# Gate and up blocks of four SwiGLU FFNs: two blocks one after the other, or chunk by chunk together

## The chip, the cores and the metric

The kernel runs on one NeuronCore of one Trainium2 chip. The metric is the device time of one launch in microseconds (us), as the median of the runs shown. The profile is of one execution.

## The reference

The computation is two layers over a state of 512 tokens (256 latent, 256 context) by 1024, in fp32. Each layer is a half-step SwiGLU FFN, a mixer of attention, gated convolution and pooling, and another half-step FFN. In the last FFN only the 256 latent tokens are left. What the change touches is the first product of each FFN:

```python
D_MODEL = 1024; SEQ = 256; CTX_LEN = 256; DEPTH = 2; D_FF = 2816

def _swiglu(x, w_gu, w_down):
    g, u = jnp.split(x @ w_gu, 2, axis=-1)
    return (jax.nn.silu(g) * u) @ w_down

for l in range(DEPTH):
    mod = (silu_c @ w_mod[l] + b_mod[l]).reshape(B, N_MOD, D_MODEL)   # shifts, scales and gates
    ...
    h = h + 0.5 * m[2][:, None] * _swiglu(_modulate(_rms(h, norm_w[l, 0]), m[0], m[1]),
                                          ffn1_w_gu[l], ffn1_w_down[l])
    ...                                                               # mixer, then the second FFN
```

The product `silu_c @ w_mod[l]`, the modulation, is also computed inside the kernel, in the shadow of the FFNs.

## The kernel before, in words

**Data.** The state is held transposed, 1024 features as 8 chunks of 128 partitions, tokens along the free axis (`w` = 512, or 256 in the last FFN). All products are fp32 made of three reduced-precision ones: a weight block and the activations are each split into a high part and the rest (`whi`, `wlo`, `xh`, `xl`), and the helper `three` (lines 1159 to 1163) issues high × high, high × low, low × high into one PSUM bank. A matmul has one 128 × 128 weight tile and up to 512 moving columns.

**Weights.** They come as a stream of 320 blocks of 512 KB, in the order in which they are used. SP loads block n into `raw` (line 332) once block n − 5 is finished (`block_done`, ring of 5). `raw` and `wlo` are the same memory. ACT copies it to `whi` (line 396), which waits for block n − 4 to be finished, since `whi` has 4 slots. DVE then subtracts, giving `wlo` (line 683). PE waits for that with `lo_done`.

**An FFN.** Its first stage, gate/up, has 44 blocks: gate block 2j and up block 2j+1 are pair j (j from 0 to 21). `column_block` (line 1165) multiplies one block: 8 chunks of three matmuls, 24 in a row into one bank, and signals `block_done` with the last. Blocks 0 to 2 go through `first_blocks` as the normalised activations arrive, the other 41 through `column_block`, in banks 0, 1, 2, 3 in turn. Before the first block of a pair PE waits with `mul_done` until the pair two before has been read out of its two banks. When both blocks of pair j are finished, ACT applies SiLU to the gate bank (line 409) and DVE multiplies with the up bank (`hidden`, line 731). ACT makes the high part of the product `ah` (line 414) and DVE the low part `al` (`hidden_low`, line 738). The second stage, down, has 22 blocks (`down`, line 1260): each goes through four banks, three matmuls in a bank and then the next, with the same moving columns. The third bank of its first block waits for `hidden` of the last pair (line 1267).

**The modulation.** 36 units of half a modulation vector. A unit's weights come in four loads of 512 KB on POOL's queue (line 354), two in flight. DVE multiplies and accumulates them for both condition vectors in four parts (`mod_pair`, lines 704 and 708, four instructions of 512 columns each), then 8 small matmuls of PE sum over the partitions (`mod_sums`, line 1222, waiting for `mod_acc`), which are recorded as 16. In the first three FFNs (f = 0, 1, 2) the gate/up stage carries 11, 11 and 9 units: unit i − 1 of the stage is summed inside block 4i + 1, before its third chunk.

**The order around it** is written out by hand for each engine. Within one pair j it is:

```python
# ACT: split_next(2j), hidden_high(j-1), split_next(2j+1), silu(j)
# DVE: split_next(2j), hidden_low(j-1), mod_pair(unit, e), split_next(2j+1), hidden(j), mod_pair(unit, e+1)
```

`split_next(n)` splits block n + 4. A unit takes two such iterations of DVE (its parts e = 0, 1 and then 2, 3), so its last part stands behind `hidden` of pair 2i − 1. Engines follow this order whatever is ready.

Of the kernel before, what the change touches and what calls it, by code (L numbers as in the profile page):

```python
# [28 lines left out]
DC = D // P  # L29
# [16 lines left out]
RING = 5  # L46
SPL = 4
GU = 2 * FC
# [27 lines left out]
FIRST = 3  # L76
# [21 lines left out]
def program(nc, wstream, wmod, cols, x_t, out):  # L98
    with ExitStack() as ctx:
        def sb(name, shape, dt=F32):  # L100
            return ctx.enter_context(nc.sbuf_tensor(name, shape, dt))

        def sem(name):
            return ctx.enter_context(nc.semaphore(name))
# [5 lines left out]
        wlo = sb("wlo", [P, RING, TILES, P], F32R)  # L110
        whi = sb("whi", [P, SPL, TILES, P], F32R)
        h = sb("h", [P, DC, T])
        xh = sb("xh", [P, DC, T], F32R)
        xl = sb("xl", [P, DC, T], F32R)
# [52 lines left out]
        ps = ctx.enter_context(nc.psum_tensor("ps", [P, 8, T], F32))  # L167

        def col(name, i=0, n=1):
            a = COLS[name][0] + i  # L170
            assert i + n <= COLS[name][1]
            return K[:, a:a + n]
# [6 lines left out]
        lo_done = sem("lo_done")  # L179
        block_done = sem("block_done")  # L180
# [24 lines left out]
        mul_done = sem("mul_done")  # L205
# [38 lines left out]
        def width(m):  # L244
            return T if m < 5 else S

        def streams(m):
            return width(m) // S
# [4 lines left out]
        def staggered(m):  # L253
            return 0 < m < 5
# [23 lines left out]
        def xstep(m, d, s):  # L278
            return XT[m] + DC * s + d + 1
# [28 lines left out]
        def unit_steps(u):  # L308
            return 2 * DC * (u - START_UNITS)
# [848 lines left out]
        def _(pe):  # L1158
            def three(out_ap, hi_w, lo_w, hi_x, lo_x, start, stop):

                pe.matmul(out_ap, hi_w, hi_x, start=start, stop=False)  # L1161
                pe.matmul(out_ap, hi_w, lo_x, start=False, stop=False)  # L1162
                return pe.matmul(out_ap, lo_w, hi_x, start=False, stop=stop)  # L1163

            def column_block(n, bank, a, b, last=True, between=None):


                pe.wait_ge(lo_done, n + 1)
                for c in range(DC):
                    if c == 2 and between:  # L1170
                        between()
                    ins = three(ps[:, bank, a:b], whi[:, n % SPL, c, :], wlo[:, n % RING, c, :],
                                xh[:, c, a:b], xl[:, c, a:b], c == 0, c == DC - 1)
                if last:
                    ins.then_inc(block_done, 1)
                return ins

            def first_blocks(m, n):


                for s in range(streams(m)):
                    a, b = s * S, (s + 1) * S
                    last = s == streams(m) - 1
                    for c in range(DC):
                        pe.wait_ge(xl_done, xstep(m, c, s))
                        for q in range(2):
                            if c == 0:
                                pe.wait_ge(lo_done, n + q + 1)
                            ins = three(ps[:, FIRST_BANKS[m][q], a:b], whi[:, (n + q) % SPL, c, :],
                                        wlo[:, (n + q) % RING, c, :], xh[:, c, a:b], xl[:, c, a:b],  # L1190
                                        c == 0, c == DC - 1)
                            if last and c == DC - 1:
                                ins.then_inc(block_done, 1)
                    if staggered(m) and s == 0:
                        norm_stat(m, 1)
                    column_block(n + 2, FIRST_BANKS[m][2], a, b, last)
# [19 lines left out]
            def mod_sums(f, u):  # L1216

                pe.wait_ge(mod_acc, unit_steps(u + 1))
                for v in range(2):
                    r = 2 * (u - UNIT_AT[f][0]) + v  # L1220
                    for j in range(HN // P):
                        ins = pe.matmul(ps[32 * j:32 * j + 32, ROWS_BANK, 0:P], col("pick", 31 - r, 32),  # L1222
                                        macc[:, v, j * P:(j + 1) * P], start=r == 0,
                                        stop=u + 1 == SET_ENDS[f] and v == 1)
                ins.then_inc(mod_sum, 1)

            def mod_turn(f):

                pe.wait_ge(mod_rows, f + 1)
                pe.transpose(ps[:, TURN_BANK, 0:P], mrows[:, :], col("ident", 0, P)).then_inc(mod_turned, 1)  # L1230
# [11 lines left out]
            def ffn(l, st):  # L1242
                f = 2 * l + (st == 2)
                m = 3 * l + st
                n0 = PER_LAYER * l + (0 if st == 0 else FFN + MIX)
                w = width(m)
                u0, nu = UNIT_AT.get(f, (0, 0))
                F0 = FC * f

                first_blocks(m, n0)  # L1250
                for i in range(GU // 4):
                    for e in range(FIRST if i == 0 else 0, 4):
                        if e % 2 == 0 and i:

                            pe.wait_ge(mul_done, F0 + 2 * i + e // 2 - 1)
                        sums = e == 1 and 1 <= i <= nu
                        column_block(n0 + 4 * i + e, e, 0, w,
                                     between=(lambda u=u0 + i - 1: mod_sums(f, u)) if sums else None)

                def down(hf, b, order, banks, a=0, z=w, first=0, final=HALF - 1, parts=0):  # L1260

                    n = n0 + GU + HALF * hf + b
                    pe.wait_ge(lo_done, n + 1)
                    for r, d in order:
                        if hf == 0 and b == 0 and r == 0:

                            pe.wait_ge(mul_done, F0 + FC - (d < 2))
                        src = (2 * b + r) * T
                        ins = three(ps[:, banks[d], a:z], whi[:, n % SPL, 4 * r + d, :],
                                    wlo[:, n % RING, 4 * r + d, :], ah[:, src + a:src + z], al[:, src + a:src + z],  # L1270
                                    b == first and r == 0, b == final and r == 1)
                        if r == 1 and d < parts:
                            ins.then_inc(part_done, 1)
                    return ins

                by_row = [(r, d) for r in range(2) for d in range(4)]
                by_bank = [(r, d) for d in range(4) for r in range(2)]
                pairs = [(r, d) for g in range(2) for r in range(2) for d in (2 * g, 2 * g + 1)]
                for b in range(HALF):

                    pe.wait_ge(al_done, F0 + 2 * b + 2)
                    down(0, b, pairs if b == 0 else by_row, DN_BANKS[0]).then_inc(block_done, 1)
                    if nu == GU // 4 and b == 1:
                        mod_sums(f, u0 + nu - 1)
                    if f == 0 and b == 6:
                        mod_sums(f, LATE_UNIT)
                    if nu and b == 8:
                        mod_turn(f)
                if nu:

                    pe.wait_ge(mod_col, SET_ENDS[f])
                    pe.wait_ge(mod_rows, f + 1)
                if not staggered(m + 1):
                    for b in range(HALF - 1):
                        down(1, b, by_row, DN_BANKS[1]).then_inc(block_done, 1)
                    down(1, HALF - 1, by_bank, DN_BANKS[1], parts=3).then_inc(block_done, 1)
                    return
                main = HALF - TAIL
                for b in range(main):
                    down(1, b, by_row, DN_BANKS[1], final=main - 1).then_inc(block_done, 1)  # L1300

                pe.wait_ge(h_done, H0[m] + JOINT)
                for b in range(main, HALF - 1):
                    down(1, b, by_row, DN_BANKS[0], 0, S, first=main)
                down(1, HALF - 1, by_bank, DN_BANKS[0], 0, S, first=main, parts=4)

                pe.wait_ge(h_done, H0[m] + 2 * JOINT)
                for b in range(main, HALF - 1):
                    down(1, b, by_row, DN_BANKS[1], S, T, first=main).then_inc(block_done, 1)
                    if b == main:  # L1310
                        norm_stat(m + 1, 0)
                down(1, HALF - 1, by_bank, DN_BANKS[1], S, T, first=main, parts=3).then_inc(block_done, 1)
# [291 lines left out]
```

## Time and profile before

| | |
|---|---|
| time, median of 3 runs | 1734.02 us (1733.18 to 1736.59) |
| span of the profiled execution, first to last instruction | 1731.9 us |
| PE matmuls | busy 1670.1 us (96%), 9475 instructions |
| VectorE (DVE) | busy 1085.4 us (63%) |
| ScalarE (ACT) | busy 610.1 us (35%) |
| DMA | 249.42 MB, mean 144 GB/s |
| granted clock of TensorE | 0.988 of full speed |

The times of the runs do not say which of them was profiled; its span lies 2.1 us under their median. PE is TensorE, its weight loads are recorded apart (PEld) and overlap the matmuls. Matmuls overlap each other, so the distance between their starts is what one costs, not its duration. In the rows, L12 is line 12 of the kernel, and "[idle before <-releaser]" is how long the engine had nothing to do before the row and what ended that.

### The profile page before, as it was taken

The numbers are of one execution on the slowest core, as the hardware profiler recorded it, in microseconds if no ns is written. First come the engines' busy times: TensorE is split into PE (matmuls) and PEld (weight loads), VectorE is DVE, ScalarE is ACT, GpSimd is POOL, SyncE is SP. The second block draws the span as 40 slices with busy tenths as digits, with TensorE's granted clock in tenths as the row PEclk, the third lists the DMA queues.
The fourth block names the chain that finished last, engine by engine and source line by source line (L and its number), as shares of the span: only waits on it lengthen the run. The fifth ranks groups of instructions, "written<-read, shape, count | busy, mean of one in ns | idle before, by whom it ended". The sixth has DMA issues, their size and how long they took to land.

```text
span 1731.9 us, 23714 instructions
## 1 busy us (share of the span) xinstructions
PE 1670.1 (96%) x9475; PEld 1416.9 (82%) x9475; DVE 1085.4 (63%) x1652; ACT 610.1 (35%) x917; POOL 84.9 (5%) x150
## 2 busy tenths in 40 slices
PE   3999999999999999999999999999999999979999
PEld 1888887889877897888888887888888987979999
DVE  2877777435668577787753387777423477755544
ACT  3422222123545452222222152222222365544432
POOL 0000000000000100000000000000000000000000
PEclk9999999999999999999999999999999999989999
DMA  9355555432221225565543245555323332335554
GB/s 362 123 182 189 183 187 188 154 96 86 89 71 49 86 98 169 184 195 184 182 157 98 74 142 171 186 193 179 105 96 97 97 99 80 131 119 183 183 168 149
DMA packets 69881, 249.42 MB, mean 144 GB/s; under 512 B 7440, under 2 KB 8464, under 8 KB 69776
## 3 DMA queue, kind: packets, MB, share of 16 engines
q1 hardware_dynamic: 51344, 180.83, 31.8%
q0 software_dynamic: 18432, 67.12, 11.8%
q8 instruction: 75, 1.23, 0.3%
q14 instruction: 30, 0.25, 0.0%
HBM read 246.87 MB, written 1.05 MB: 143 GB/s over the span
## 4 chain that ended last, share of the span: by engine, by line
PE 90%; DVE 4%; DMA 2%; issue 2%; ACT 1%; SPq 1%; POOLq 0%; POOL 0%; DVEq 0%; ACTq 0%
PE ps L1161 29%; PE ps L1162 28%; PE ps L1163 28%; DMA raw<-wstream 2%; DVE shared_a L708 1%; PE ps L1222 1%; PE ps L1364 1%; ACT whi L396 1%; PE ps L1396 1%; PE ps L1324 1%; DVE wlo L683 1%; SPq L326 1%; PE ps L1378 0%; SPq L322 0%; DVE nmax L1006 0%
## 5 line engine op out<-in xcount | busy, mean ns | idle before, releaser
L683 DVE TENSOR_TENSOR wlo<-raw,whi 128x1024 fp32r<-128x1024 f32 x320 | 393.7, 1230 | 576.0 <-ACT whi L396 574.4
L1161 PE MATMUL ps<-xh,whi 128*128 128x512 f32 (+1 forms) x1956 | 692.6, 354 | 8.6 <-DVE xl L793 5.1
L1162 PE MATMUL ps<-xl,whi 128*128 128x512 f32 (+1 forms) x1956 | 676.2, 346 | 0.0
L1163 PE MATMUL ps<-xh,wlo 128*128 128x512 f32 (+1 forms) x1956 | 675.6, 345 | 0.0
L396 ACT ACTIVATE whi<-raw 128x1024 fp32r<-128x1024 f32 x320 | 338.6, 1058 | 910.8 <-PE ps L1163 776.9
L1161 PEld LDWEIGHTS ps<-xh,whi 128*128 128x128 f32 x1956 | 373.7, 191 | 66.5 <-issue 12.8
L1162 PEld LDWEIGHTS ps<-xl,whi 128*128 128x128 f32 x1956 | 374.0, 191 | 46.2 <-issue 3.8
L1163 PEld LDWEIGHTS ps<-xh,wlo 128*128 128x128 f32 x1956 | 373.5, 191 | 45.1
L708 DVE SCALAR_TENSOR_TENSOR shared_a<-wm,cs,shared_a 128x512 f32<-128x512 f32 x448 | 307.6, 746 | 0.0
L1161 PE MATMUL ps<-ah,whi 128*128 128x512 f32 (+1 forms) x800 | 274.6, 343 | 3.7 <-DVE shared_b L731 3.7
L1162 PE MATMUL ps<-al,whi 128*128 128x512 f32 (+1 forms) x800 | 273.0, 341 | 0.0
L1163 PE MATMUL ps<-ah,wlo 128*128 128x512 f32 (+1 forms) x800 | 272.9, 341 | 0.0
L1161 PEld LDWEIGHTS ps<-ah,whi 128*128 128x128 f32 x800 | 152.4, 190 | 22.9 <-DVE shared_b L731 5.2
L1163 PEld LDWEIGHTS ps<-ah,wlo 128*128 128x128 f32 x800 | 152.4, 190 | 17.0
L1162 PEld LDWEIGHTS ps<-al,whi 128*128 128x128 f32 x800 | 152.5, 191 | 16.7
L354 POOL DMA_DIRECT2D wm<-wmod x126 | 66.8, 530 | 892.1 <-DVEq L711 884.5
L461 ACT ACTIVATE shared_a<-h 128x256 f32<-128x256 f32 (+1 forms) x64 | 31.6, 498 | 81.7 <-DVE h L750 73.4
L750 DVE SCALAR_TENSOR_TENSOR h<-ps,gcol,h 128x256 f32<-128x256 f32 x104 | 45.6, 477 | 20.8 <-PE ps L1163 20.7
L731 DVE TENSOR_TENSOR shared_b<-shared_b,ps 128x512 f32<-128x512 f32 (+1 forms) x88 | 54.1, 615 | 2.5 <-ACT shared_b L409 2.5
L738 DVE TENSOR_TENSOR al<-shared_b,ah 128x512 fp32r<-128x512 f32 (+1 forms) x88 | 54.4, 619 | 1.5 <-ACT ah L414 1.2
L477 ACT ACTIVATE xh<-shared_b,modc 128x256 fp32r<-128x256 f32 x88 | 42.2, 504 | 31.1 <-DVE shared_b L785 31.1
L414 ACT ACTIVATE ah<-shared_b 128x512 fp32r<-128x512 f32 (+1 forms) x88 | 49.5, 563 | 9.9 <-DVE shared_b L731 9.9
(106 smaller groups left out, 798.9 us busy)
## 6 DMA issues: line engine op xcount, KB each, us to landing
raw<-wstream SPq DMA_DIRECT2D x320, 512.0 KB, 3.5
wm<-wmod POOLq DMA_DIRECT2D x128, 512.0 KB, 4.7
wm<-wmod SPq DMA_DIRECT2D x3, 2048.0 KB, 20.5
h<-x_t SPq DMA_DIRECT2D x1, 2048.0 KB, 11.4
wm<-wmod SPq DMA_DIRECT2D x2, 1024.0 KB, 20.4
out_t<-h SPq DMA_DIRECT2D x8, 128.0 KB, 2.7
K<-cols SPq DMA_DIRECT2D x1, 939.0 KB, 13.8
K<-cols SPq DMA_DIRECT2D x1, 268.5 KB, 3.0
```

Of the source, the lines that this page charges most:

```text
L354: pool.dma_start(wm[:, c, :, :].rearrange("p a n -> p (a n)"), wmod[bass.ds(i * 2 + c, 1)].rearrange("a p n -> p (a n)"))\
L396: act.activation(whi[:, n % SPL, :, :].rearrange("p a b -> p (a b)"), raw[:, n % RING, :], ACT.Copy)\
L414: act.activation(ah[:, j * T:j * T + w], af[:, j % 2, 0:w], ACT.Copy).then_inc(ah_done, 1)
L477: act.activation(xh[:, d, s * S:(s + 1) * S], xt[:, (g - 1) % 4, :], ACT.Identity, bias=modc[:, N_MOD * l + 3 * st, d, s:s + 1]).then_inc( ...
L683: dve.tensor_tensor(wlo[:, n % RING, :, :].rearrange("p a b -> p (a b)"), raw[:, n % RING, :], whi[:, n % SPL, :, :].rearrange("p a b -> p ...
L708: ins = dve.scalar_tensor_tensor(acc, src, sc, acc, ALU.mult, ALU.add)
L731: dve.tensor_tensor(af[:, j % 2, 0:w], sil[:, j % 2, 0:w], ps[:, gu_bank(f, 2 * j + 1), 0:w], ALU.mult)\
L738: dve.tensor_tensor(al[:, dst], af[:, j % 2, 0:w], ah[:, dst].bitcast(F32), ALU.subtract)\
L750: ins = dve.scalar_tensor_tensor(h[:, d, v * S:(v + 1) * S], ps[:, bank, v * S:(v + 1) * S], gcol[:, m, d, v:v + 1], h[:, d, v * S:(v + 1) ...
L1161: pe.matmul(out_ap, hi_w, hi_x, start=start, stop=False)
L1162: pe.matmul(out_ap, hi_w, lo_x, start=False, stop=False)
L1163: return pe.matmul(out_ap, lo_w, hi_x, start=False, stop=stop)
```

## The change

In the gate/up stage, blocks 4 to 43 are no longer multiplied one after the other. The new function `column_pair` takes a gate block and its up block together. For each of the 8 chunks it goes through `xh` with `whi`, `xh` with `wlo`, `xl` with `whi`, and issues each for the gate block into bank `bank` and for the up block into bank `bank + 1`. Both blocks must be split before it starts (`lo_done` at n + 2). The last two matmuls of the pair signal `block_done`, one each. The sums of a modulation unit stand ahead of chunk 5 of the pair (30 of its 48 matmuls before them), where they stood ahead of the third chunk of its second block (24 + 6 before them). Block 3 stays a `column_block`, and the other engines' programs are as before.

```diff
+                def column_pair(n, bank, between=None):
+                    pe.wait_ge(lo_done, n + 2)
+                    for c in range(DC):
+                        if c == 5 and between:
+                            between()
+                        for x, lo in ((xh, False), (xh, True), (xl, False)):
+                            for q in range(2):
+                                wt = wlo[:, (n + q) % RING, c, :] if lo else whi[:, (n + q) % SPL, c, :]
+                                ins = pe.matmul(ps[:, bank + q, 0:w], wt, x[:, c, 0:w],
+                                                start=c == 0 and x is xh and not lo, stop=c == DC - 1 and x is xl)
+                                if c == DC - 1 and x is xl:
+                                    ins.then_inc(block_done, 1)
+
                 first_blocks(m, n0)
-                for i in range(GU // 4):
-                    for e in range(FIRST if i == 0 else 0, 4):
-                        if e % 2 == 0 and i:
-
-                            pe.wait_ge(mul_done, F0 + 2 * i + e // 2 - 1)
-                        sums = e == 1 and 1 <= i <= nu
-                        column_block(n0 + 4 * i + e, e, 0, w,
-                                     between=(lambda u=u0 + i - 1: mod_sums(f, u)) if sums else None)
+                column_block(n0 + FIRST, FIRST, 0, w)
+                for i in range(1, GU // 4):
+                    for e in (0, 2):
+
+                        pe.wait_ge(mul_done, F0 + 2 * i + e // 2 - 1)
+                        sums = e == 0 and i <= nu
+                        column_pair(n0 + 4 * i + e, e,
+                                    between=(lambda u=u0 + i - 1: mod_sums(f, u)) if sums else None)
```

## Rows read from the trace of the kernel before

**Rows 1.** The page, part 4: shares of the chain that ended last, by engine.

```profile
PE 90%; DVE 4%; DMA 2%; issue 2%; ACT 1%; SPq 1%; POOLq 0%; POOL 0%; DVEq 0%; ACTq 0%
```

**Rows 2.** Timeline of PE, a block with sums: start us, us, engine, line, operation, tiles, count.

```profile
168.96 0.39 PE L1161 MATMUL ps<-xh,whi 128*128 128x512 f32 x1
...
170.41 0.64 PE L1222 MATMUL ps<-shared_a,K 128*32 128x128 f32 x16
...
175.20 0.39 PE L1161 MATMUL ps<-xh,whi 128*128 128x512 f32 x1
```

**Rows 3.** Timeline of DVE, then ACT, beside the block of rows 2.

```profile
164.87 1.23 DVE L683 TENSOR_TENSOR wlo<-raw,whi 128x1024 fp32r<-128x1024 f32 x1 [0.96 <-ACT whi L396]
...
166.61 2.73 DVE L708 SCALAR_TENSOR_TENSOR shared_a<-wm,cs,shared_a 128x512 f32<-128x512 f32 x4
...
170.31 1.23 DVE L683 TENSOR_TENSOR wlo<-raw,whi 128x1024 fp32r<-128x1024 f32 x1 [0.97 <-ACT whi L396]
...
169.22 1.06 ACT L396 ACTIVATE whi<-raw 128x1024 fp32r<-128x1024 f32 x1 [3.89 <-PE ps L1163]
```

**Rows 4.** Timeline of DVE in the first FFN, while it works without a gap.

```profile
69.31 1.23 DVE L683 TENSOR_TENSOR wlo<-raw,whi 128x1024 fp32r<-128x1024 f32 x1
...
71.05 2.73 DVE L708 SCALAR_TENSOR_TENSOR shared_a<-wm,cs,shared_a 128x512 f32<-128x512 f32 x4
...
73.93 1.23 DVE L683 TENSOR_TENSOR wlo<-raw,whi 128x1024 fp32r<-128x1024 f32 x1
...
75.08 0.68 DVE L731 TENSOR_TENSOR shared_b<-shared_b,ps 128x512 f32<-128x512 f32 x1
...
75.67 2.73 DVE L708 SCALAR_TENSOR_TENSOR shared_a<-wm,cs,shared_a 128x512 f32<-128x512 f32 x4
```

**Rows 5.** Timeline of PE: first sums of three FFNs, and the block after each.

```profile
78.46 1.08 PE L1222 MATMUL ps<-shared_a,K 128*32 128x128 f32 x16 [4.15 <-DVE shared_a L708]
...
84.84 0.39 PE L1161 MATMUL ps<-xh,whi 128*128 128x512 f32 x1
...
660.22 1.08 PE L1222 MATMUL ps<-shared_a,K 128*32 128x128 f32 x16 [3.79 <-DVE shared_a L708]
...
667.47 0.39 PE L1161 MATMUL ps<-xh,whi 128*128 128x512 f32 x1
...
1039.87 0.64 PE L1222 MATMUL ps<-shared_a,K 128*32 128x128 f32 x16 [3.77 <-DVE shared_a L708]
...
1046.25 0.39 PE L1161 MATMUL ps<-xh,whi 128*128 128x512 f32 x1
```

**Rows 6.** Windows: column blocks, down blocks, narrow FFN. Stretch, length, busy (xcount), PEclk, DMA share, GB/s.

```profile
1237.00:1257.00 20.00, 20.00 (x90) 16.57 (x89) 6.98 (x8) 6.25 (x8) 0.00 (x0) 1.00 0.33 103
314.00:338.00 24.00, 24.00 (x108) 19.87 (x107) 14.10 (x18) 4.24 (x4) 2.12 (x4) 1.00 0.52 176
1610.00:1650.00 40.00, 40.00 (x336) 40.00 (x335) 21.42 (x28) 18.87 (x28) 0.00 (x0) 1.00 0.56 183
```

**Rows 7.** The chain in order of time, last block of the narrow gate/up stage.

```profile
1658.94 3.94 DMA raw<-wstream
```

**Rows 8.** DMA issues from 90 to 290: count, KB each, median us to landing.

```profile
raw<-wstream SPq DMA_DIRECT2D x36, 512.0 KB, 3.5
wm<-wmod POOLq DMA_DIRECT2D x36, 512.0 KB, 4.8
```

**Rows 9.** Windows behind the pauses that end at 660.22 and 1665.60.

```profile
662.00:664.00 2.00, 2.00 (x7) 1.54 (x6) 2.00 (x5) 0.00 (x0) 0.00 (x0) 0.50 0.83 254
...
1666.00:1668.00 2.00, 2.00 (x11) 2.00 (x11) 0.43 (x1) 0.00 (x0) 0.00 (x0) 0.50 0.00 0
```

**Rows 10.** Timeline of PE: the matmuls that end other pauses.

```profile
302.25 0.50 PE L1161 MATMUL ps<-ah,whi 128*128 128x512 f32 x1 [0.35 <-DVE shared_b L731]
...
1546.34 0.38 PE L1161 MATMUL ps<-xh,whi 128*128 128x256 f32 x1 [0.95 <-DVE shared_b L731]
...
1665.60 0.51 PE L1161 MATMUL ps<-ah,whi 128*128 128x256 f32 x1 [2.37 <-DVE shared_b L731]
```

## The prediction

> **What bounds the kernel now.** I read the chain that ended last first [rows 1]: 90% of it is TensorE (PE), and no other engine has more than 4%. So a matmul saved is time saved, and a pause of PE is time lost. Whether PE pauses depends on the engines that feed it, so next I read one steady period of the gate/up stage, where most of the changed code runs. The block that carries the modulation sums [rows 2]: its first matmul is at 168.96, the sums (L1222) come at 170.41, which is 1.45 after it, and the next block begins at 175.20, 4.79 after the sums. Beside it [rows 3], DVE's splits start at 164.87 and 170.31, 5.44 apart, as the blocks of PE end: 24 matmuls of 0.2267. The last four multiply-adds of the unit (L708, `mod_pair`) run from 166.61 for 2.73, to 169.34. The sums may start then, and PE reaches them at 170.41: a slack of 1.07 us. That number is what the change has to live with. Two delays for later: ACT starts its split 0.26 after the next block's first matmul (169.22 − 168.96), and DVE 1.09 after ACT (170.31 − 169.22).
>
> Three first units already show this wait failing. DVE when it works without a gap [rows 4]: from the split at 69.31 to the modulation pair at 71.05 it is 1.74, on to the next split 2.88, to `hidden` (L731) 1.15, to the second modulation pair 0.59, and that lasts 2.73, to 78.40. The sums come 0.06 later, at 78.46 [rows 5], and PE had been idle for 4.15.
>
> **The matmuls themselves.** The change issues the same 48 matmuls for a pair of blocks in another order, with a weight load each as before. Could the order make them cheaper? In the down stage, every third matmul already goes to another bank with the same moving columns as the one before it (`xh` or `ah` of L1163, then of L1161, with d changed). In the windows of rows 6 the column blocks start 90 matmuls in 20.00 us and the down blocks 108 in 24.00: 0.222 us each in both. So neither alternating banks nor sharing columns is worth anything that this trace can show, and I enter 0. The bounds: a gain down to pure streaming at the granted 2.4 GHz (512 columns, 0.2133; 256 columns, 0.1067) would be 0.0134 on 2,880 matmuls (120 blocks of 24 in the three wide FFNs) and 0.0123 on 960 (40.00/336 = 0.119 [rows 6] less 0.1067), so 38.6 + 11.8 = 50 us. For a loss I take the opposite of that as the end, 0.01 on each, 38 us; rows 6 lie at neither.
> The Trainium skill (TensorE: Matmul & The Clock Gate, "Back-to-back issue gap") gives N/2.4 + 2.5 ns, 216 ns at 512 columns and 109 at 256; this trace has 227 and 119. If the new order brought the kernel to the page's gap, an estimate from it is 2,880 × 11 ns + 960 × 10 ns = 41 us of gain; nothing in rows 6 points there, and the sum does without it.
>
> **When blocks are finished.** Before, gate block 2j of pair j ended 5.44 before up block 2j+1. Now both end together; the gate block's last matmul is the second to last of the pair. What waits for `block_done` of 2j is ACT's split of block 2j+4, DVE's split behind it, and SP's load of block 2j+5. All of them start nearly a block later, and everything behind them in DVE's fixed order moves as well: `hidden_low`, the first modulation pair, the second split, `hidden`, the second modulation pair. Let T be the first matmul after pair j. ACT starts the first split at T + 0.26 − 0.227 = T + 0.03, DVE at T + 1.12. By rows 4 the first modulation pair then starts at T + 2.86, the second split at 5.74, `hidden` at 6.89, the second modulation pair at 7.48, and it ends at 10.21. Before, only one split, `hidden` and the second pair lay behind T: T was 168.96 − 5.44 = 163.52 and the end 169.34, T + 5.82.
>
> Is anything else late? The load of 2j+5 is issued at T − 0.06 and takes 3.5 to 3.94 [rows 7, 8], so it is there by T + 3.9; ACT then lets DVE in at T + 5.0, before 5.74, hidden by 0.7. The next pair but one needs both its blocks split (5.74 + 1.23 = 6.97) and `hidden` of j (6.89 + 0.68 + 0.06 = 7.63) by T + 10.88: hidden with 3.2 to spare. If that cover goes, the narrow FFN shows the price (term 4). DVE's whole iteration (10.21) fits in the 10.88 of a pair too.
>
> **Term 1, the sums.** They now stand ahead of chunk 5 of pair 2i, 30 matmuls after T: T + 6.80, plus the 0.09 that rows 2 have at the same place (1.45 − 6 × 0.2267), T + 6.89, which is where they stood before (5.44 + 1.45). They need the modulation pair that ends at 10.21, so they start at T + 10.27: PE pauses 3.38. How often: units with sums in the loop are i = 1 to 10, 1 to 10 and 1 to 9, 29 in all; the first of each FFN waits already and does not change, since blocks 0 to 3 and their splits keep their times. 26 new pauses × 3.38 = 87.9 us.
>
> **Term 2, the clock.** After such pauses the granted clock is at 0.50, the 1.2 GHz level: so behind the one that ends at 660.22, and behind the one of the narrow FFN that ends at 1665.60 [rows 9, 10]. From the start of the sums to the next block normally takes 4.79. In rows 5 it takes 84.84 − 78.46 = 6.38, 667.47 − 660.22 = 7.25 and 1046.25 − 1039.87 = 6.38: dearer by 1.59, 2.46, 1.59, mean 1.88. Those pauses were about 4 us and mine is 3.4, but the one of 2.37 at 1665.60 dropped the clock too; behind the 0.95 of 1546.34 the blocks came at full rate. So each of my 26 is charged 1.88: 48.9 us. Bounds: 0 and 2.46 each (0 and 64).
>
> **Term 3, the end of each gate/up stage.** The third bank of the first down block waits for `hidden` of the last pair. Before, it started at 302.25 [rows 10] with 0.35 of idle time, counted from the modelled end of a matmul, 0.39 − 0.227 = 0.16 behind its turn; so 0.51 late, and the 12 matmuls ahead of it take 2.72: T + 3.23. Now it starts at T + 7.63: 4.40 more, and the pause of 4.9 costs the clock too: 6.3, in two FFNs. In the third, where the last pair has no modulation pair beside it, the load sets it: T + 3.9, DVE 1.11 later, `hidden` at 6.15 to 6.83, PE at 6.9: 3.7 + 1.9 = 5.6. In the narrow one the load is issued at T + 0.04 and takes 3.94 [rows 7]; DVE at 5.09, `hidden` at 6.24 and taken as 0.41 long (between half and all of the 0.68 of rows 4), PE at T + 6.71. Before, T was 1658.94 − 0.16 + 24 × 0.119 = 1661.64 and PE went on at 1665.60, T + 3.96: 2.7 more, its clock drop is there already. Sum 12.6 + 5.6 + 2.7 = 20.9 us.
>
> **Term 4, the narrow FFN.** A pair of 256 columns takes 48 × 0.119 = 5.71. Pair j+2 needs `hidden` of j (its bank's reader) at T + 6.71, and its turn comes at T + 5.71: 1.00 of pause. After it the next pair is in time, so the pause comes before every second pair, 9 times: 9.0 us, without a clock drop at that length [rows 10].
>
> **Sum.** 87.9 + 48.9 + 20.9 + 9.0 = 166.7 on a span of 1731.9: 1898.6. The median of the runs shown is 2.1 above this span, so 1901.
>
> **Rivals.** (a) The pauses come, but are too short for the clock: less 29 × 1.9 = 55 us, 1846. For it: 3.4 is shorter than the three of about 4. Against it: 2.4 was enough once. (b) The loads come in twos and hold each other up. The narrow FFN moves 183 GB/s at a DMA share of 0.56 [rows 6], so 327 at full share, 1.6 us for 0.52 MB. If the first of two lands 1.6 later, at T + 5.5, DVE's second split starts at 6.55 in place of 5.74: 0.8 × 26 = 21, plus 1.6 × 9 = 14 in the narrow FFN and 4 at the stage ends: 1940. Against it: loads beside modulation loads of the same size already land in 3.5, and those in 4.8 [rows 8].
> The Trainium skill (Trainium Kernel Development and Optimization, "Key Constraints") says that transfers of all issuing queues run on the same 16 DMA engines and interleave; by that the first of two loads lands nearly with the second, which is case (b).
> (c) The other side: matmuls in alternating banks with shared columns cost 0.0134 us less, and no pause comes because DVE is done in time. All 50 us are kept: 1684. It decides if DVE's iteration ends by T + 6.8, 3.4 us earlier than rows 4 have it; I see nothing that makes it so, and rows 6 speak against the cheaper matmul. With the pauses standing, what lies ahead of the sums is lost in the wait, about 35 us stay, and the time is 1866. (d) Nothing moves, the later block end is hidden altogether: 1734.
>
> **How the numbers follow.** Forecast 0.70, its own range 1882 to 1922 (a clock drop of 1.3 to 2.5 a pause, loads up to half of case b). (a) 0.10. (b) 0.12. (c) 0.05, of which 0.03 at 1684 and 0.02 at 1866. (d) 0.03. A measurement of this kernel can tell about 0.2% (3.5 us) from no change. Slower: 0.70 + 0.10 + 0.12 + 0.02 = 0.94; same 0.03; faster 0.03. The range takes in (b) and reaches to the edge of (a): 1850 to 1942.
>
> **What would show it.** In the profile of the changed kernel: L1222 waits for DVE's L708 29 times, some 3.4 each; the sums come every 22.6 + 3.4 + 1.9 = 27.9 us; the clock line lies below 9 in the three wide FFNs; the number of matmuls (9475) and their pitch stay; the third bank of the first down block starts 7.6 after T. Wrong would be: a pitch of 0.215 in the pairs (c), a granted clock of 1.00 behind the pauses (a), DVE's second split waiting for ACT in the modulation iterations (b), no wait at L1222 (d).

## The result and the profile after

The changed kernel takes 1902.82 us (median of 4 runs, 1901.67 to 1908.44) against 1734.64 for the kernel before on the same chip. The ratio is 1.097, with a 95% interval of 1.0955 to 1.0991: slower by 168 us, where 1901 had been forecast. The profiled execution is the longest of the four (1908.44); its span is 1906.7.

The page of the changed kernel: busy time, the granted clock in 40 slices, the chain that ended last by engine and by line.

```profile
span 1906.7 us, 23714 instructions
PE 1728.6 (91%) x9475; PEld 1455.3 (76%) x9475; DVE 1085.2 (57%) x1652; ACT 609.6 (32%) x917; POOL 84.6 (4%) x150
...
PEclk9989989999999998998899999999999999989999
...
PE 73%; DMA 11%; DVE 10%; ACT 3%; issue 3%; SPq 1%; POOLq 0%; POOL 0%; DVEq 0%; ACTq 0%
```

The number of matmuls is what it was, 9475, and DVE and ACT are as busy as before in microseconds. The chain has changed hands [rows 1]: PE held 90% of it and holds 73% now; DMA went from 2% to 11% and DVE from 4% to 10%. The clock line falls to 8 in five slices of the first two wide FFNs (it was 9 there) and stays at 9 in the third. The forecast wanted it below 9 in all three, which its own numbers did not give: 1.9 us lost in a period of 27.9 is a mean of 0.93, and the mean in the gate/up stages of all three is 0.92.

Who made PE wait in the changed kernel (total, times, longest):

```profile
PE ps L1222 <- DVE shared_a L708: 105.6, 29, 4.2
...
PE ps L1161 <- DVE shared_b L731: 18.5, 4, 5.0
PE ps L1260 <- DVE shared_b L731: 7.8, 11, 1.8
```

The three lines are the three places of the forecast: the sums of 29 units (L1222); the third bank of the first down block, once in each of the four FFNs (L1161); and the pairs of the narrow FFN (L1260). Next, one such period at close range. First DVE, then PE, in the changed kernel (start, length, instruction; in brackets idle time and what ended it).

```profile
182.85 1.23 DVE L683 TENSOR_TENSOR wlo<-raw,whi 128x1024 fp32r<-128x1024 f32 x1 [2.31 <-ACT whi L396]
183.99 0.68 DVE L738 TENSOR_TENSOR al<-shared_b,ah 128x512 fp32r<-128x512 f32 x1
184.59 2.73 DVE L708 SCALAR_TENSOR_TENSOR shared_a<-wm,cs,shared_a 128x512 f32<-128x512 f32 x4
187.53 1.23 DVE L683 TENSOR_TENSOR wlo<-raw,whi 128x1024 fp32r<-128x1024 f32 x1 [0.20 <-ACT whi L396]
188.67 0.68 DVE L731 TENSOR_TENSOR shared_b<-shared_b,ps 128x512 f32<-128x512 f32 x1
189.26 2.73 DVE L708 SCALAR_TENSOR_TENSOR shared_a<-wm,cs,shared_a 128x512 f32<-128x512 f32 x4
```

```profile
180.36 0.62 PE L1260 MATMUL ps<-xh,whi 128*128 128x512 f32 x2
...
187.16 0.62 PE L1260 MATMUL ps<-xh,whi 128*128 128x512 f32 x2
...
188.07 0.61 PE L1260 MATMUL ps<-xl,whi 128*128 128x512 f32 x2
192.06 1.08 PE L1222 MATMUL ps<-shared_a,K 128*32 128x128 f32 x16 [3.37 <-DVE shared_a L708]
...
195.60 0.62 PE L1260 MATMUL ps<-xh,whi 128*128 128x512 f32 x2
```

From one block end DVE now works off two splits, `hidden_low`, two modulation pairs and `hidden` in a row, from 182.85 to 191.99; the sums follow at 192.06. In the kernel before, the first half of that work ran while the up block was multiplied [rows 3]. Two more things can be read here. The bracket at 187.53 says that DVE stood for 0.20 there, waiting for ACT. Of that 0.15 is there also when DVE works without a gap [rows 4], so this split came only 0.05 later than the forecast had it; over the 26 new pauses the mean is 0.31. And the matmuls: from 180.36 to 187.16 there are 15 rows of two, 30 matmuls, so 6.80/30 = 0.2267 us from one start to the next, exactly as before. The Trainium skill (TensorE: Matmul & The Clock Gate, "Back-to-back issue gap") has 216 ns for 512 columns by its formula, and about 131 ns for a sustained stream with weight loads. The trace agrees with neither, in the old order or the new, and its 227 ns decides here.

Why ACT was late: it waited for a load. ACT beside it, and the DMA issues of the stretch 100 to 340 (count, KB, median us to landing), changed kernel.

```profile
186.43 1.06 ACT L396 ACTIVATE whi<-raw 128x1024 fp32r<-128x1024 f32 x1 [3.10 <-DMA raw<-wstream]
```

```profile
raw<-wstream SPq DMA_DIRECT2D x32, 512.0 KB, 4.7
```

In the median a weight block took 3.5 to land [rows 8] and takes 4.7 now that two are asked for at once. In the periods of the 26 new pauses, the first of the two takes 3.6 to 5.5 (median 4.9) and the second about 5.8. The first one is what the second split needs, and its landing gives that split's delay to 0.01: the delay is the time by which it lands after T + 4.63 (T is the first matmul after a pair, as in the prediction), from 0.00 to 0.81. The Trainium skill (Trainium Kernel Development and Optimization, "Key Constraints") says that transfers interleave on the same 16 DMA engines; this agrees, at some 1.2 to 1.4 us for the first of two.

The pause at the end of a gate/up stage, in the changed kernel: the first matmul of the third bank in the first wide FFN, and the clock behind it (windows; the clock is the third number from the end).

```profile
358.76 0.50 PE L1161 MATMUL ps<-ah,whi 128*128 128x512 f32 x1 [4.87 <-DVE shared_b L731]
```

```profile
358.50:362.00 3.50, 3.24 (x9) 2.54 (x10) 3.35 (x6) 0.63 (x1) 0.00 (x0) 0.60 0.41 150
362.00:364.00 2.00, 2.00 (x9) 1.67 (x8) 0.19 (x1) 0.54 (x1) 0.53 (x1) 0.84 0.32 66
```

The idle time of 4.87 stands where 0.35 stood before [rows 10].

### The profile page after: what moved, and what is told of

The parts are those of the page before. It is cut to its first block, busy times and chain, and to the rows that moved or that the text cites. A ratio compares the mean times of both kernels' runs of the same rounds, so it can differ in the third digit from the quotient of the medians.

```text
span 1906.7 us, 23714 instructions
## 1 busy us (share of the span) xinstructions
PE 1728.6 (91%) x9475; PEld 1455.3 (76%) x9475; DVE 1085.2 (57%) x1652; ACT 609.6 (32%) x917; POOL 84.6 (4%) x150
## 4 chain that ended last, share of the span: by engine, by line
PE 73%; DMA 11%; DVE 10%; ACT 3%; issue 3%; SPq 1%; POOLq 0%; POOL 0%; DVEq 0%; ACTq 0%
PE ps L1260 30%; PE ps L1161 13%; PE ps L1162 12%; PE ps L1163 12%; DMA raw<-wstream 11%; DVE shared_a L708 5%; ACT whi L396 3%; DVE wlo L683 2%; PE ps L1222 2%; DVE shared_b L731 1%; PE ps L1379 1%; PE ps L1411 1%; PE ps L1339 1%; SPq L326 1%; SPq L322 0%
## 5 line engine op out<-in xcount | busy, mean ns | idle before, releaser
L1260 PE MATMUL ps<-xh,whi 128*128 128x512 f32 (+1 forms) x1280 | 384.1, 383 | 7.8 <-DVE shared_b L731 7.8
L1260 PE MATMUL ps<-xh,wlo 128*128 128x512 f32 (+1 forms) x1280 | 378.0, 378 | 0.0
L1260 PE MATMUL ps<-xl,whi 128*128 128x512 f32 (+1 forms) x1280 | 373.4, 374 | 0.0
L708 DVE SCALAR_TENSOR_TENSOR shared_a<-wm,cs,shared_a 128x512 f32<-128x512 f32 x448 | 307.5, 746 | 0.0
L1161 PE MATMUL ps<-ah,whi 128*128 128x512 f32 (+1 forms) x800 | 276.7, 346 | 18.5 <-DVE shared_b L731 18.5
L1260 PEld LDWEIGHTS ps<-xh,whi 128*128 128x128 f32 x1280 | 239.1, 198 | 58.8 <-DVE shared_b L731 10.3
L1260 PEld LDWEIGHTS ps<-xh,wlo 128*128 128x128 f32 x1280 | 241.9, 198 | 42.3
L1260 PEld LDWEIGHTS ps<-xl,whi 128*128 128x128 f32 x1280 | 240.9, 197 | 42.3
L1161 PE MATMUL ps<-xh,whi 128*128 128x256 f32 (+1 forms) x676 | 222.5, 329 | 7.7 <-DVE xl L793 5.1
L1162 PE MATMUL ps<-xl,whi 128*128 128x256 f32 (+1 forms) x676 | 209.6, 310 | 0.0
L1163 PE MATMUL ps<-xh,wlo 128*128 128x256 f32 (+1 forms) x676 | 209.5, 310 | 0.0
L1161 PEld LDWEIGHTS ps<-ah,whi 128*128 128x128 f32 x800 | 153.7, 192 | 38.3 <-DVE shared_b L731 20.0
L1161 PEld LDWEIGHTS ps<-xh,whi 128*128 128x128 f32 x676 | 130.6, 193 | 21.8 <-issue 6.7
L1222 PE MATMUL ps<-shared_a,K 128*32 128x128 f32 x512 | 29.3, 366 | 105.6 <-DVE shared_a L708 105.6
```

What stands on the lines that cost most here:

```text
L708: ins = dve.scalar_tensor_tensor(acc, src, sc, acc, ALU.mult, ALU.add)
L1260: ins = pe.matmul(ps[:, bank + q, 0:w], wt, x[:, c, 0:w], start=c == 0 and x is xh and not lo, stop=c == DC - 1 and x is xl)
```

## The experiments

All times are compared with the kernel before on the same chip, 1734.05 and 1734.10 us. Two theories stand against each other first. **Late signal**: the matmuls cost what they did, and all of the loss comes from the gate block being reported finished one block later. **Order**: alternating banks, or demanding two split blocks at once, costs the time by itself.

### Late signal with the old order

```diff
-                        column_block(n0 + 4 * i + e, e, 0, w,
-                                     between=...)
+                        ins = column_block(n0 + 4 * i + e, e, 0, w, last=i == 0,
+                                           between=...)          # between: as before
+                        if i and e % 2:
+                            ins.then_inc(block_done, 2)
```

> The kernel before, with its matmul order, but in blocks 4 to 43 of each gate/up stage the gate block is signalled finished only together with its up block. Theory (late signal): the order of the matmuls costs nothing, the later signal costs everything, so the time is that of the changed kernel, 1903 (1897 to 1909), with 29 waits of L1222 on L708, about 3.7 each, and 1.9 of half clock behind each. Rival (order): alternating banks or the wait for two split blocks costs the time; then this kernel stays at 1735.

Measured: 1916.87 us, ratio 1.1054 (1.1035 to 1.1072). Who made PE wait in it:

```profile
PE ps L1222 <- DVE shared_a L708: 111.6, 29, 4.7
PE ps L1161 <- DVE shared_b L731: 28.6, 15, 5.3
```

The order theory falls: its order is the old one, and the loss is all there. But it is 14 us slower than the changed kernel, outside of the range expected. One difference in the signals was left: in the changed kernel the gate block's last matmul is the second to last of the pair, here its signal comes with the last.

### The signal one matmul earlier

```diff
+                    if early and c == DC - 1:
+                        pe.matmul(ps[:, bank, a:b], whi[...], xh[:, c, a:b], start=False, stop=False)
+                        pe.matmul(ps[:, bank, a:b], whi[...], xl[:, c, a:b], start=False, stop=False)\
+                            .then_inc(block_done, 1)
+                        ins = pe.matmul(ps[:, bank, a:b], wlo[...], xh[:, c, a:b], start=False, stop=True)
+                        continue
...
+                        column_block(n0 + 4 * i + e, e, 0, w, last=i == 0 or e % 2 == 1, early=i > 0 and e % 2 == 1,
```

> As late_signal (sequential matmul order, gate block signalled late), but the gate block's signal sits on the second to last matmul of the up block, where the changed kernel has it too. Theory: the 14 us between late_signal (1917) and the changed kernel (1903) come from that signal being one matmul (0.227) later, in 26 sums and the narrow FFN; so this one gives 1903 (1897 to 1909). Rival: the alternating order saves something; then it stays near 1917.

Measured: 1906.51 us, ratio 1.0995 (1.0974 to 1.1017), an interval that overlaps that of the changed kernel (1.0955 to 1.0991). Who made PE wait at the sums in it:

```profile
PE ps L1228 <- DVE shared_a L708: 105.4, 29, 4.8
```

The changed kernel has 105.6 there. Old order with the changed kernel's signals gives the changed kernel's waits at the sums, and its time to within 4 us. So 10 of the 14 us were one matmul of delay in the signal; whether the remaining 4 are the order or chance, these runs cannot tell.

### Only the split late, only the load late

Two things wait for the gate block: ACT's split of block 2j+4 and SP's load of block 2j+5. Each was made late alone, with the old order and PE's signals as before (`gate(n)` is 1 for the gate blocks 4 to 42 of each FFN).

```diff
-                    act.wait_ge(block_done, n - SPL + 1)
+                    act.wait_ge(block_done, n - SPL + 1 + gate(n - SPL))
```

> The kernel before; only ACT's split of block 2j+4 waits for the up block 2j+1 in place of the gate block 2j. The loads start when they always did. Theory: DVE's iteration is serial behind T, without any hold-up by a load: sums at T + 10.27, pause 3.38, so 26 x (3.38 + 1.9) = 137; stage ends 12.6 + 2.5 + 0.2; nothing in the narrow FFN (hidden done at T + 4.2, before 5.7). 1734.6 + 152 = 1887. Rival (loads): the later load is what holds DVE; then 1735.

```diff
-                    sp.wait_ge(block_done, n - RING + 1)
+                    sp.wait_ge(block_done, n - RING + 1 + gate(n - RING))
```

> The kernel before; only SP's load of block 2j+5 waits for the up block 2j+1 in place of the gate block 2j. Theory: the load comes at T + 0.16 and lands 3.9 to 4.7 later, DVE's second split starts at T + 5.2 to 6.0, the sums at T + 9.7 to 10.5: a pause of 2.8 to 3.6, 26 x (3.2 + 1.9) = 133, stage ends 10 + 5.6 + 2.7, narrow FFN 9: 1734.6 + 160 = 1895 (1884 to 1906); either waiter alone costs nearly all. Rival (only the split matters): 1735 to 1750. Rival (only the load matters): 1903.

Measured: 1889.25 us with the split late (ratio 1.0899, 1.0881 to 1.0917) and 1879.38 with the load late (1.0848, 1.0813 to 1.0882). Either alone costs 155 and 145 of the 168 us; they are two doors to the same wait, not two terms to be added. Both rivals, that one of them alone matters, fall. PE's waits at the sums, and the median landing of the weight loads from 100 to 340 (in these two kernels lines behind 245 are numbered 5 higher). With the split late:

```profile
PE ps L1227 <- DVE shared_a L713: 104.3, 29, 4.8
...
raw<-wstream SPq DMA_DIRECT2D x34, 512.0 KB, 3.5
```

With the load late:

```profile
PE ps L1227 <- DVE shared_a L713: 89.7, 29, 4.8
...
raw<-wstream SPq DMA_DIRECT2D x34, 512.0 KB, 5.0
```

The load alone came out below its range (1884 to 1906), and the clock is the larger part of that. The 26 new pauses run from 2.4 to 4.1, with a mean of 3.0 where 3.2 had been expected, which is 4 us in all; the time lost behind a pause was 1.5 in the mean and not 1.9, which is 11 us.

With the split late the pause is the same every time. The last matmul ahead of the sums and the sums, and DVE's last modulation pair, in that kernel:

```profile
215.45 0.39 PE L1168 MATMUL ps<-xh,wlo 128*128 128x512 f32 x1
```

```profile
219.38 0.65 PE L1227 MATMUL ps<-shared_a,K 128*32 128x128 f32 x16 [3.54 <-DVE shared_a L713]
```

```profile
216.59 2.74 DVE L713 SCALAR_TENSOR_TENSOR shared_a<-wm,cs,shared_a 128x512 f32<-128x512 f32 x4
```

219.38 − 215.45 − 0.227 is 3.70, less the normal 0.09: 3.61, and so it is at 26 of the 29 sums to 0.01, all but the first of each FFN. That is the 3.38 of the forecast plus the 0.227 by which this signal comes later than the pair's. The loads land in 3.5 here, and nothing holds DVE up. This settles what the varying part in the changed kernel is, together with the landings read there: its loads, asked for in twos. Each of its 26 new pauses is 3.38 plus the delay of the second split, to 0.01.

### The new order without the wait

The changed kernel, with the sums moved behind the place where DVE is done.

```diff
-                        sums = e == 0 and i <= nu
-                        column_pair(n0 + 4 * i + e, e,
+                        sums = e == 2 and i <= nu
+                        column_pair(n0 + 4 * i + e, e, 1,          # ahead of chunk 1, not 5
```

> The changed kernel, with the sums of a unit moved from ahead of chunk 5 of pair 2i to ahead of chunk 1 of pair 2i+1, at T + 10.88 + 1.36, after DVE is done (T + 10.2 to 10.6). Theory: the 29 waits and the half clock behind them go, those of the first units too (17.6 of the kernel before); what stays is stage ends 20.9 and narrow FFN 9: 1734.6 - 17.6 + 29.9 = 1747 (1740 to 1755). Rival (order): the matmul order costs by itself, the time stays over 1850. Rival (DVE then waits for the sums before the next unit and is late for the splits): over 1770, with waits of PE on L683 or L731.

Measured: 1747.90 us, ratio 1.0077 (1.0061 to 1.0094). L1222 no longer waits for L708 at all; what PE waits for in this kernel besides the start-up, the norms and the mixers is

```profile
PE ps L1161 <- DVE shared_b L731: 18.5, 5, 5.5
PE ps L1260 <- DVE shared_b L731: 7.0, 10, 1.9
```

the stage ends and the narrow FFN, as forecast. One call moved by four chunks of a pair (24 matmuls, 5.4 us) makes the changed kernel faster by 155 us. Some 18 of these are the three first waits, which the kernel before has as well, so about 137 of the 168 us are given back.

### The pause filled with work

Is the time behind a pause lost to the clock? The changed kernel with 16 matmuls, whose result nothing reads, ahead of each unit's sums.

```diff
                         if c == 5 and between:
+                            for k in range(FILL):                  # FILL = 16
+                                pe.matmul(ps[:, 6, 0:w], whi[:, n % SPL, k % DC, :], xh[:, k % DC, 0:w],
+                                          start=k == 0, stop=k == FILL - 1)
                             between()
```

> The changed kernel with 16 matmuls of 512 columns more ahead of each unit's sums, into bank 6, which nothing reads there: 3.63 us of work in the place of the pause. Theory (half of each loss is the clock): the sums wait as long as before for DVE, but TensorE is busy, the granted clock stays at 1.00, and the 1.9 behind each of the 29 sums goes: 1903 - 29 x 1.9 = 1848 (1840 to 1860), with 0.1 to 0.7 of pause left. Rival (what follows the sums is slow for another reason, a queue that has to fill again): 1903 or more.

Measured: 1857.90 us, ratio 1.0713 (1.0695 to 1.0730). 464 matmuls more and 45 us less. Its windows behind a filled pause, and its waits:

```profile
183.00:187.00 4.00, 4.00 (x31) 3.12 (x31) 0.00 (x0) 0.00 (x0) 0.53 (x1) 1.00 0.45 131
```

```profile
PE ps L1223 <- DVE shared_a L709: 5.8, 6, 2.7
```

The clock stays at 1.00, and from the start of the sums to the 19th matmul after it it is 4.79 to 4.83 at 28 of the 29 sums, as in the kernel before. The rival falls. The time is 10 us above the point expected (inside of the range). Part of that is that DVE was late beyond the filler: what is left of the pauses adds up to 6.8, where 3.71 less the filler's 3.63 would leave 2.3 over the 29. Five of these waits (0.4 to 2.7) are in the second FFN, the longest with a clock drop of its own (1.6).

### The narrow FFN alone

```diff
-                for i in range(1, GU // 4):
+                for i in range(1, GU // 4 if w == S else 1):       # pairs; wide FFNs use the old loop
```

> The new order in the fourth FFN alone (256 columns, no modulation), the other three as before. Theory: 8.9 of small pauses and 2.7 at the stage end: 1734 + 11.6 = 1746 (1742 to 1750). Rival (the loads in pairs cost this stage much more or the cheaper matmul shows here, where its share is largest): over 1755 or under 1734.

Measured: 1745.95 us, ratio 1.0064 (1.0047 to 1.0081), 11.9 above the kernel before, where 11.6 was expected. PE's waits at the pairs:

```profile
PE ps L1260 <- DVE shared_b L731: 6.9, 11, 1.6
```

### Faster than both

The reading of [rows 5] pointed to a version that has nothing to do with pairs: the three first units of the kernel before wait already.

```diff
-                        sums = e == 1 and 1 <= i <= nu
-                        column_block(n0 + 4 * i + e, e, 0, w,
+                        sums = e == (2 if i == 1 else 1) and 1 <= i <= nu
+                        column_block(n0 + 4 * i + e, e, 0, w, at=1 if i == 1 else 2,   # chunk of the sums
```

> The kernel before, not the changed one, with only the first unit's sums of each FFN moved one block later (ahead of the second chunk of block 6 in place of the third of block 5). Theory: its three waits at L1222 (4.2, 3.9, 3.8) and the half clock behind them (1.6, 2.5, 1.6) go: 1734 - 17.6 = 1716.5 (1714 to 1720), ratio 0.990. Rival: DVE is 4 us behind at that point and the wait turns up at the second unit's sums, PE pauses there: 1728 to 1734.

Measured: 1716.27 us, ratio 0.9897 (0.9880 to 0.9913), faster than the kernel before by 17.8, where 17.6 was expected. The first sums of it:

```profile
79.18 0.39 PE L1163 MATMUL ps<-xh,wlo 128*128 128x512 f32 x1
79.50 0.64 PE L1222 MATMUL ps<-shared_a,K 128*32 128x128 f32 x16
80.07 0.50 PE L1161 MATMUL ps<-xh,whi 128*128 128x512 f32 x1
```

No pause, and none at the second unit's sums: DVE catches up in between, 0.8 us in each block (5.44 of PE against 4.62 of DVE, [rows 3, 4]). The rival falls. The changed kernel with its sums moved (1747.90) is still 32 us slower than this one: that is what the new order costs at the stage ends and in the narrow FFN.

## Why the prediction was right

Point by point, with sizes from the profiled execution. Both kernels record 9475 matmuls, stage by stage in the same numbers, so the k-th start of one can be set against the k-th of the other, and the difference read stage by stage. A pause is the distance of the sums from the matmul before less 0.227 and less the normal 0.09; the clock is the distance from the sums to the 19th matmul behind them (start of the next pair or block) less the normal one. The normal one is 4.82, the mean over the 26 undisturbed periods of the kernel before, and not the 4.79 of [rows 2].

| term | forecast | measured |
|---|---|---|
| 26 new pauses at the sums | 87.9 (3.38 each) | 95.8 (3.69 each) |
| clock behind them | 48.9 (1.88 each) | 48.6 (1.86 each) |
| stage ends, with the clock | 20.9 | 14.8 pauses + about 5.1 clock |
| narrow FFN | 9.0 | 10.0 |
| sum | 166.7 | 174.3 of 174.8 between the two spans |

In the first two rows the measured total is that of the 29 sums of the changed kernel less that of the three waits of the kernel before; the figure in brackets is the mean of the 26 new ones.

**The matmuls** were entered at 0. Right: 0.2267 us each before and after, and old order with new signals is within 4 us of the changed kernel.

**The sums** were the place, 29 times, with the 3 first ones there before. The size was 0.31 short. The term that was mis-sized is the load: "lands after 3.5 to 3.94, hidden by 0.7" took rows of loads asked for singly. In twos the median is 4.7, and DVE's second split waits for it: at 25 of the 26 new pauses it came late. That was the prediction's own sign of rival (b), which so came in part, at some 40% of its price (0.31 of 0.8). Where loads come singly, the runs gave the forecast's 3.38 + 0.227 to the hundredth.

**The clock** was charged from three pauses of about 4 us and one of 2.4. The mean held, though single pauses cost 1.3 to 2.9; the filler run shows it to be the clock, since there it is gone with the pause.

**The stage ends**: the added idle time is 4.52, 4.61, 3.07 and 2.62, against 4.40, 4.40, 3.65 and 2.7. The third came out shorter than forecast. The clock behind the three wide ones cost 1.6 each, where 1.9 was charged.

**The narrow FFN**: the number of small pauses was right (10 behind the start-up, forecast 9), their sizes, from start to start, run from 0.5 to 1.9 where 1.0 was the forecast for each. With a smaller one of 0.2 they come to 8.9; the matmul behind each of them is 0.1 late too, which the forecast left out, and that makes 10.0 of it.

Rivals (a), (c) and (d) did not happen. That the median (1902.82) lies within 2 us of the forecast is in part luck: the terms of the profiled execution come to 8 us more than forecast, and that execution is the longest of the four. What is not explained is why one of four runs of the changed kernel is 5.6 us above the median of the four; the varying landing of loads would do it, but that was only argued.

## What to carry to other kernels

A reordering that leaves every matmul in place can still cost a tenth of the time, if it moves the moment when a buffer is reported free: list who waits for each signal, and add up in the waiter's fixed order what is serial behind it now. A consumer that needs a result 1 us after it is ready, in a period of 22.6, is one signal away from a pause. Here moving that consumer by 5.4 us was repair enough. In this kernel many pauses of TensorE of some 3.7 us cost the pause plus about half again for the clock (3.69 and 1.86 in the mean).

## What the runs showed of the hardware that was not expected

**The clock drop is not the same for equal pauses.** Over the 29 sums of the changed kernel, pauses of 3.4 to 4.3 us cost 1.3 to 1.6 us more behind them 21 times, and 2.7 to 2.9 eight times. Nor does the length decide it: in the kernel with the split late 26 pauses are 3.61 long, and 20 of them cost 1.4 to 1.6, the other six 2.9. A few cost nothing: one of 3.78 in the kernel with the signal one matmul earlier, and two of 2.61 and 2.80 in the one with the load late. The windows of those two kernels right behind such a pause (of 3.78, then of 2.61); the clock is the third number from the end:

```profile
1151.00:1157.00 6.00, 6.00 (x40) 4.86 (x37) 0.21 (x1) 1.30 (x2) 0.53 (x1) 1.00 0.37 102
```

```profile
246.00:252.00 6.00, 5.39 (x37) 4.36 (x38) 4.50 (x7) 0.00 (x0) 1.06 (x2) 1.00 0.27 90
```

So a single pause could not be priced here by its length. Over the 29 sums of a kernel the mean cost ran from 1.5 (load late) to 2.0 (late signal).

**One matmul of delay in a signal was worth 10 us** (1916.87 against 1906.51): 0.227 in 26 sums is 5.9. Between the two profiled executions, which lie 12.9 apart, the pauses at the sums differ by 6.1, the clock behind them by 7.0, the narrow FFN by 1.2 and the stage ends by 1.4 the other way. With one execution of each, how much of the clock's part belongs to the delay is not shown.
